# Low parts of normalised tiles moved from GpSimd to VectorE, the first heads' query rotation moved behind the key tile's evictions, and the start's square sums and warm-up regrouped

## What is computed

```python
# per layer; x is (tokens, 1024)
xn = rmsnorm(x, ln_g)
q, k, v, z_a, x_b, z_b, g_a, g_b = split(xn @ w_in)
q = rope(q);  k = rope(k) * 256 ** -0.5            # 4 heads of 256, values of 512
ret, S_new = retention(q, k, v, S)                  # decayed attention plus a recurrent state
o_a = group_norm(ret) * silu(z_a)
o_b = rglru(causal_conv(x_b)) * silu(z_b)
x = x + (sigmoid(g_a) * (o_a @ w_a) + sigmoid(g_b) * (o_b @ w_b)) @ w_o
# after the two layers: y = rmsnorm(x, final_gain); the new states are outputs too
```

## Time and profile before

| | us |
|---|---|
| median of 3 runs (1937.81 to 1938.79) | 1938.37 |
| the profiled execution, its own time | 1938.32 |
| its span, first to last instruction | 1936.5 |
| PE busy | 1918.5 (99%) |
| DVE busy | 1181.5 (61%) |
| ACT busy | 742.3 (38%) |
| POOL busy | 265.2 (14%) |
| mean granted TensorE clock | 0.999 |

### The profile page before, as it was taken

One profiled execution on the slowest core, in us unless ns is written; L12 is line 12 of the kernel. 1 busy time (PEld: TensorE's weight loads), 2 busy tenths in 40 slices (PEclk: granted clock), 3 DMA queues, 4 the chain that ended last, 5 costly groups with the idle time before them and its releaser, 6 DMA issues.

```text
span 1936.5 us, 32128 instructions
## 1 busy us (share of the span) xinstructions
PE 1918.5 (99%) x13184; PEld 1797.3 (93%) x13184; DVE 1181.5 (61%) x2008; ACT 742.3 (38%) x1149; POOL 265.2 (14%) x375
## 2 busy tenths in 40 slices
PE   8999999999999999999999999999999999999998
PEld 8889898898899999999998988988988999999997
DVE  8665665565666887424486655656556678853345
ACT  5332322323336766422343223233223367754223
POOL 2221120120231200000021201202102422000000
PEclk9999999999999999999999999999999999999999
DMA  6434533453343333322255335534534533342222
GB/s 216 134 115 163 178 125 125 162 169 112 130 155 99 105 105 107 123 77 77 88 170 168 126 126 169 168 112 134 178 116 137 167 98 104 101 135 79 84 81 81
DMA packets 105856, 247.01 MB, mean 128 GB/s; under 512 B 10830, under 2 KB 51134, under 8 KB 105326
## 3 DMA queue, kind: packets, MB, share of 16 engines
q1 hardware_dynamic: 78590, 149.74, 25.0%
q0 software_dynamic: 26976, 95.22, 14.9%
q10 hardware_dynamic: 144, 0.00, 0.0%
HBM read 186.10 MB, written 49.12 MB: 121 GB/s over the span
## 4 chain that ended last, share of the span: by engine, by line
PE 86%; DVE 5%; ACT 4%; DVEq 1%; DMA 1%; ACTq 1%; issue 1%; SPq 0%
PE bank L1624 21%; PE bank L1626 20%; PE bank L1625 20%; PE bank L1694 5%; PE bank L1696 5%; PE bank L1695 5%; PE last L1712 1%; PE last L1694 1%; PE last L1695 1%; PE last L1696 1%; PE bank L1852 1%; PE sums L1729 1%; DVE ct L1416 1%; DVE w_lo L462 1%; DVE rr L1469 1%
## 5 line engine op out<-in xcount | busy, mean ns | idle before, releaser
L1624 PE MATMUL bank<-xn_hi,w_hi 128*128 128x296 f32 (+1 forms) x2432 | 727.5, 299 | 0.2
L1626 PE MATMUL bank<-xn_lo,w_hi 128*128 128x296 f32 (+1 forms) x2432 | 722.4, 297 | 0.0
L1625 PE MATMUL bank<-xn_hi,w_lo 128*128 128x296 f32 (+1 forms) x2432 | 721.5, 297 | 0.0
L1624 PEld LDWEIGHTS bank<-xn_hi,w_hi 128*128 128x128 f32 x2432 | 457.3, 188 | 5.9 <-issue 4.3
L1625 PEld LDWEIGHTS bank<-xn_hi,w_lo 128*128 128x128 f32 x2432 | 457.8, 188 | 0.4
L1626 PEld LDWEIGHTS bank<-xn_lo,w_hi 128*128 128x128 f32 x2432 | 456.8, 188 | 0.0
L462 DVE TENSOR_TENSOR w_lo<-w_raw,w_hi 128x1024 fp32r<-128x1024 f32 x245 | 300.3, 1228 | 184.8 <-ACT w_hi L454 177.1
L454 ACT ACTIVATE w_hi<-w_raw 128x1024 fp32r<-128x1024 f32 x245 | 257.7, 1055 | 362.2 <-DMA w_raw<-in_w_units 357.7
L1624 PE MATMUL bank<-oa_hi,w_hi 128*128 128x296 f32 (+1 forms) x512 | 153.7, 300 | 0.0
L1625 PE MATMUL bank<-oa_hi,w_lo 128*128 128x296 f32 (+1 forms) x512 | 151.9, 297 | 0.0
L1626 PE MATMUL bank<-oa_lo,w_hi 128*128 128x296 f32 (+1 forms) x512 | 151.7, 296 | 0.0
(11 more groups left out here) (286 smaller groups left out, 3083.7 us busy)
## 6 DMA issues: line engine op xcount, KB each, us to landing
w_raw<-in_w_units SPq DMA_DIRECT2D x215, 512.0 KB, 3.6
S<-in_state_ret POOLq DMA_DIRECT2D x64, 512.0 KB, 4.8
out_ret_s<-S POOLq DMA_DIRECT2D x64, 512.0 KB, 6.2
w_raw<-in_w_units SPq DMA_DIRECT2D x66, 256.0 KB, 3.2
vst<-v_scr SPq DMA_DIRECT2D x8, 512.0 KB, 4.1
out_ret_p<-Sp POOLq DMA_DIRECT2D x8, 512.0 KB, 5.9
v_scr<-vtok_hi SPq DMA_DIRECT2D x16, 160.0 KB
dec<-in_decay POOLq DMA_DIRECT2D x9, 264.0 KB, 5.1
```

Of the source, the lines that this page charges most:

```text
L1624: pe.matmul(ps, w_hi[:, slot, cols], x_hi, start=first, stop=False)
L1625: pe.matmul(ps, w_lo[:, slot, cols], x_hi, start=False, stop=False)
L1626: return pe.matmul(ps, w_hi[:, slot, cols], x_lo, start=False, stop=last)
```

## The change

Five edits:

- `xn_lo` is made on DVE (`norm_lo`), right behind the loop's `norm` calls, and no longer on POOL. `norm(k)` for k of 2 and more drains DVE in place of waiting for POOL's count.
- In the first head of a layer the query rotation, `qz` and `qt` leave i = 1 and go to i = 2, behind the eviction of the first key tile and behind `split_lo(2)`, mixed with `norm(2)` and `norm(3)`. ACT takes the high parts of the queries at i = 3 there. The other heads stay as they are.
- `GROUP[0]` is 2: four partial sums in layer 0, four additions on DVE where there were six, no drain ahead of them, and eight products with ones where there were four.
- The square sums stand ahead of step 9 (it was 10) in layer 0, and ahead of step 6 (it was 5) in layer 1.
- `WARM` is 12.

```diff
-WARM = 10
+WARM = 12
...
-        GROUP = [4] + [KT] * DEPTH
+        GROUP = [2] + [KT] * DEPTH
...
         def buffer(n, k):
-            return k % 2
+            return k // 2 % 2 if GROUP[n] == 2 else k % 2
...
-                    if h == 0:
-                        for k in range(KT):
-                            pool.wait_ge(xnh_ready, l * KT + k + 1)
-                            apart(pool)
-                            pool.tensor_tensor(xn_lo[:, k, :], xnf[:, k % 2, :], xn_hi[:, k, :].bitcast(f32), SUB)\
-                                .then_inc(xn_ready, 1)
-                        pool.drain()
...
-                        if i == 2:
+                        if i == (2 if h else 3):
                             act.wait_ge(qk_ready, hh * 2 + 1)
                             act.activation(qt_hi[:, :, :], qt[:, :, :], ACT.Copy)
...
             for k in range(KT):
-                dve.drain()
                 add_square(0, k)
...
+                def norm_lo(k):
+
+                    dve.wait_ge(xnh_ready, l * KT + k + 1)
+                    dve.tensor_tensor(xn_lo[:, k, :], xnf[:, k % 2, :], xn_hi[:, k, :].bitcast(f32), SUB)\
+                       .then_inc(xn_ready, 1)
...
                 def norm(k):
 
                     if k >= 2:
-                        dve.wait_ge(xn_ready, l * KT + k - 1)
+                        dve.drain()
...
+                            if i == 3:
+                                rotated(2, turn, 0)
+                            if i == 1 and h:
+                                rotated(0, turn, first)
+                                queries_apart()
+                            if i == 3 or i == 1 and h:
                                 dve.drain().then_inc(qk_ready, 1)
...
                         if i not in (7, 9):
                             split_lo(dve, "R", l, h, i)
                         if h == 0:
-                            for k in {2: (2, 3), 3: (4, 5), 4: (6,), 5: (7,)}.get(i, ()):
+                            if i == 1:
+                                norm_lo(0)
+                                norm_lo(1)
+                            if i == 2:
+                                norm(2)
+                                rotated(0, rot, first)
+                                norm(3)
+                                queries_apart()
+                                dve.drain().then_inc(qk_ready, 1)
+                                norm_lo(2)
+                                norm_lo(3)
+                            for k in {3: (4, 5), 4: (6,), 5: (7,)}.get(i, ()):
                                 norm(k)
+                            for k in {3: (4, 5), 4: (6,), 5: (7,)}.get(i, ()):
+                                norm_lo(k)
...
-                        project_first("R", l, h, xg_ready, 0, raw, *((10, 5, True) if l == 0 else (5, 3)))
+                        project_first("R", l, h, xg_ready, 0, raw, *((9, 5, True) if l == 0 else (6, 3)))
```

More of the change, by code:

```diff
@@ L1165, in _, with rotated @@
                             dve.drain()
-                            if i % 2:
-                                a = first if i == 1 else 0
+                            def rotated(at, turn, a):
                                 dve.tensor_tensor(qk[:, at, a:], qk[:, at, a:], turn[:, 0, a:], SUB)
@@ L1172, in _, with queries_apart @@
                                 dve.drain()
-                            if i == 1:
+                            def queries_apart():
                                 dve.wait_ge(const_in, 32)
```

## The result

The changed kernel takes 1946.53 us (median of 6 runs, 1944.73 to 1947.47); the kernel before, run beside it, 1939.12 (1937.81 to 1939.75). The ratio is 1.0038, 95% interval 1.0027 to 1.0048: slower by about 7.4 us, beyond the 0.2%. The profiled execution took 1944.73, its span 1942.9 where before's was 1936.5, so +6.4 us are to be explained in the trace.

The account below looks back on a forecast made before the run. PE's own work plus its gaps bound the kernel; 2.07 us in layer 0 and 4.5 in layer 1 add 6.6 to the profiled 1938.32, giving 1944.9, rounded 1945.0 us. Range 1940.5 to 1947.3.

Parts of the forecast that it names:

- What bounds the kernel: PE's own work plus its gaps; PE works 99% of the span, and longer chains behind gaps delay it.
- Z: Start of unit 6's low part in a layer's first head; forecast 48.29 in layer 0, before 49.53.
- Part 1: Two more ones products on PE at the start: 0 us, bounds 0 and +0.2.
- Part 2: Four sums in layer 0: root at 21.04, gain 1.18 us on all engines if nothing later takes it back.
- bank wait: PE's 1.8 us wait in first heads for a bank DVE frees by its query eviction; forecast gone or small.
- Part 3: DVE, i = 1 to 3: added low parts and lost POOL stretching even out; Z moves 1.18 us and -0.06 more.
- Part 4: From Z to ktok_ready: terms 7.27, 5.62 and 6.70, sum 19.59 us against 16.28, +3.31 in each layer.
- Part 5: Layer 1's sums one step later: root 0.9 us later, unit 5's load +0.4, Z +1.2.
- SP's series: SP's DMAs between ktok_ready and PE's growth: 15.17 us in layer 0, 14.86 in layer 1.
- Rival 2: Clock falls behind PE's growth waits: about 1.7 us an episode, 1946.7 with one, 1948.3 with two; chance 0.12.
- Rival 1: Not slower: the stretch from Z doesn't grow, in all 1938.3; chance 0.17 including what lies up to 1942.2.
- Rival 3: Faster: Part 2's gain is kept in both layers' chains, growth no later than PE, 1937.1; chance 0.03.

Follow-up runs that it names:

- keys6: keys_first with layer 1's square sums ahead of step 6 in place of step 5: 1936.35 us, ratio 0.9992.
- late67_q: Changed kernel, tile 6's low part behind the queries' low parts, tile 7's behind the keys', ACT's query copies behind unit 7's high part: 1938.40 us, ratio 0.9997.
- start_only: Kernel before with layer 0's start edits alone (twelve ones products, four sums, no drain, sums ahead of step 9): 1938.57 us, ratio 0.9997.
- low_only: Kernel before with the low parts made on DVE alone; rotation at i = 1, start and sums as before: 1944.15 us, ratio 1.0027.
- rot_only: Kernel before with the rotation and ACT's query copies moved in first heads, low parts left on POOL: 1942.77 us, ratio 1.0022.
- after_again: The changed kernel, unedited, profiled a second time in a single execution: 1945.72 us.
- warm10: The changed kernel with ten warm-up products in place of twelve, a single execution: 1948.09 us.
- keys_first: Changed kernel, queries' and keys' low parts and tile 7 behind ktok_ready, query copies behind unit 7's, layer 1's sums ahead of step 5: 1937.81 us, ratio 0.9996.
- fill: Changed kernel with ten unused ones products on PE before the wait for vst in first heads: 1943.35 us, ratio 1.0026.
- sums5: late67_q with layer 1's square sums back ahead of step 5: 1939.82 us, ratio 1.0005.

## Why the prediction was right, point by point

- **What bounds the kernel.** It held: DVE's busy time rose by 1.7 us, while PE's waits for `vst` grew by 4.3 (5.3 against 1.0), and 1.53 more went to the clock behind one of them. keys6 shows the other side: its way from Z is 3.9 us shorter than late67_q's in each layer, but the time fell by 2.05 us in all by the medians and 1.0 by the ratios, no more than about what PE had waited at the growths there (1.05 + 0.66).
- **Part 1.** 0 us for the end of the stretch, as said: the root stands 8.55 us behind the last copy of `xg` with ten products and with twelve. The picture ahead of it was another: in after, products run at the higher rate from 6.3 us on, not from 10, and PE then waits for `xg_lo` for the 2.0 us in place of working slowly.
- **Part 2.** ACT's last copy of `xg` to the root was 9.84 us and is 8.55, -1.29, against -1.18. The bank wait is gone in layer 0 (the 1.0 us after is one in layer 1, at 994.63). That the root came at 21.73 and not at 21.04 goes back to the inputs, which landed some 0.8 us later in this execution.
- **Part 3.** Z at 48.29 was forecast, 48.31 came, but two errors cancel in this: the root 0.69 us later than forecast, and the way from it to Z 26.58 us where I had 27.25 (27.31 before). That the two cancel is luck. The way is 27.31 in start_only, 26.96 in low_only and 25.70 in rot_only: the move of the rotation shortens it by itself, a gain for which the forecast had no term. The plain lengths returned: L1166 is 0.78 us where L1168 was 2.10. The Trainium skill's rule on the pair of ports that DVE and GpSimd share (SBUF — State Buffer, "SBUF: two separate sides") agrees with this row.
- **Part 4.** All three terms within 0.03 us, in both layers, and the two halves apart (low_only, rot_only) sum to +3.48 against the forecast +3.31. The times that the prediction gives for layer 1 (Z at 1011.5, L502 at 1031.1, the growth at 1045.9) leave out the 2.07 us of layer 0, which its total has; they came at 1013.97, 1033.62 and 1047.76.
- **Part 5, mis-sized.** Z in layer 1 was forecast 1.2 us later than before and came +0.35 (1013.97 - 3.35 - 1010.27). The root was +0.70, not +0.9. The +0.4 for unit 5's load was wrong in kind: I let it land a bit earlier in the same race, but it now leaves ahead of the state loads and holds nobody; w_lo(5) at 1004.10 has no idle time before it. I had not looked at what shares the memory with that load.
- **SP's series.** I carried over 15.17 and 14.86 us; it took 14.83 and 14.14 in the profiled execution, but 15.39 and 15.03 in after_again and 15.27 and 15.73 in warm10, so this term differs from execution to execution. The chains cost 1.82 + 2.99 = 4.8 us in the one and 2.09 + 3.77 = 5.9 in after_again, not 6.6.
- **Rival 2 came true on top.** I gave it 0.12 as a case of its own and 1.7 us per episode. It came in both executions of after that were traced, once in each, at 1.5 us. So the nearness of forecast and result is in part luck, a chain overrated and a clock rated at nothing: in the profiled execution 6.57 - 0.25 (layer 0) - 1.51 (layer 1) + 1.53 = 6.34. The step that failed is the weight of rival 2: waits of 2.6 to 3.3 us were forecast, beyond all gaps of before, and rows of gaps up to 1.7 say little of them.
- **Rival 1** needed the stretch not to grow; it grew by 3.38. **Rival 3** fell with it.

## What to carry to other kernels

Between an early result and the transfer that PE will wait for, count every instruction on every in-order engine, whether or not it is part of the chain; here the same instructions cost 8 us or nothing by their places. When a forecast opens a wait of PE longer than any that the trace shows, price the clock as well as the wait. When a load moves, look at which bulk loads of another queue it will now lead or follow.

## What the runs showed of the hardware

The clock. PE's waits before the growth and what followed, in the profiled executions: 2.54 us (low_only), 2.95 (after), 3.28 (after_again, layer 1), 3.38 and 3.99 (warm10) were followed by products 0.24 us apart; 2.38 (after, layer 1), 3.51 (after_again, layer 0) and all of 1.65 and less were not. So length alone does not decide it, and in one and the same kernel the episode falls in one layer or the other. Some executions of kernels without such waits are 2 us above their median as well (1939.59 and 1939.64 in keys_first, mean clock 0.997); none of these was traced. The Trainium skill, TensorE: Matmul & The Clock Gate, "HAM oscillation — how this bites in real kernels", describes such a return of the half clock behind waits inside a stream. The traces agree with it in that, down to waits of 2.54 and 2.95 us, but not in that it comes each time: it stayed away behind 3.51 us. Products without use in the wait kept the clock (fill).

The start has such a fall too. In low_only and warm10, both with ten warm-up products, the granted clock between 8 and 12 us is 0.65 and 0.61, in warm10 behind waits of 0.68 and 1.02 us. In rot_only, also with ten and behind waits of 0.68 and 1.12 us, it is 1.00 there, as in all ten profiles with twelve. In before, again with ten, the figure is 1.00 too, but the products start 0.245 us apart up to 10.3 us, where those with twelve start about 0.14 apart from 6.3 us on; so in before the figure doesn't show the level at the start, and the distance of the products does. In warm10 the fall cost nothing that shows at the root, which is where after has it against the last copy of `xg`.

Loads. Where a weight unit of 0.5 MB is issued just behind 2.1 MB of state loads from POOL's queue, the slowest unit load of that stretch took 8.9, 10.2 and 10.1 us to land (before, keys_first, sums5); where it is issued just ahead of them, 4.9, 4.1 and 4.9 (after, late67_q, keys6). sums5 and late67_q, and keys_first and keys6, differ in the place of layer 1's sums alone.
